# Moving a background chain twelve gather slots later, and packing its last stage into half as many slots

## What is computed

```python
def peer_ffn(x, w_query, sub_keys, u_tab, v_tab):
    q = (xc @ w_query).reshape(PEER_TBLOCK, PEER_HEADS, 2, PEER_QDIM // 2)
    s = jnp.einsum('thcd,ckd->thck', q, sub_keys)
    top_s, top_i = lax.top_k(s, K)                       # K = 16, of 128 keys
    ... best_s, best_j = lax.top_k(cand_s, K)            # of the 256 pair sums
    gate = jax.nn.softmax(best_s, axis=-1)
    act = jax.nn.gelu(jnp.einsum('thkd,td->thk', u_tab[experts], xc))
    v = v_tab[experts]
    return jnp.einsum('thk,thkd->td', (gate * act), v)

def post_norm_block(x, mix, w_out, ...):
    h = layer_norm(ALPHA * x + mix @ w_out, ln1_g, ln1_b)
    return layer_norm(ALPHA * h + peer_ffn(h, ...), ln2_g, ln2_b)

def compress(rows, pe, w1, w2):                          # one of the sparse attention's inputs
    blk = rows[:, idx] + pe[None, None, :, None, :]      # 32 rows, stride 16
    h = jax.nn.gelu(jnp.einsum('bnlgd,lde->bnge', blk, w1))
    return jnp.einsum('bnge,ef->bngf', h, w2)
```

## Time and profile before

| | us |
|---|---|
| median of three runs | 2796.11 |
| profiled execution | 2807.41 |
| its span in the trace | 2805.6 |
| mean granted TensorE clock in it | 0.793 |
| TensorE matmuls busy | 2047.4 (73%) |
| VectorE busy | 1263.4 (45%) |
| GpSimd busy | 796.6 (28%) |
| ScalarE busy | 321.8 (11%) |
| software-issued gathers (q0) | 627.05 MB, 55.2% of the 16 engines' span |
| hardware-issued loads (q1) | 332.46 MB, 31.6% |

### The profile page before, as it was taken

How to read it: one execution, slowest core, us unless ns; L and a number is a source line. 1 busy time by engine, 2 the same in 40 slices (tenths; PEclk the granted TensorE clock), 3 DMA queues, 4 the chain that set the end, 5 groups by cost and what they waited for, 6 DMA issues and landing times.

```text
span 2805.6 us, 30559 instructions
## 1 busy us (share of the span) xinstructions
PE 2047.4 (73%) x10278; PEld 1239.2 (44%) x10278; DVE 1263.4 (45%) x2354; ACT 321.8 (11%) x737; POOL 796.6 (28%) x594
## 2 busy tenths in 40 slices
PE   8999999566979997968998644554544449883334
PEld 5777665234448985746766411211110006550000
DVE  0500121233024785576795525334433354688551
ACT  0001110112012010010011002001001011011011
POOL 0000000000001143443334434225342374436762
PEclk9999999777999998988999875876766655555555
DMA  9789889753425589999999999999999999999997
GB/s 395 290 349 368 343 305 361 284 188 141 189 77 216 208 297 392 373 370 365 388 384 356 354 348 412 389 379 380 414 373 421 422 421 421 421 416 387 422 422 302
DMA packets 213165, 963.81 MB, mean 344 GB/s; under 512 B 23761, under 2 KB 89298, under 8 KB 122258
## 3 DMA queue, kind: packets, MB, share of 16 engines
q0 software_dynamic: 84512, 627.05, 55.2%
q1 hardware_dynamic: 128354, 332.46, 31.6%
q10 hardware_dynamic: 144, 2.36, 0.2%
HBM read 955.28 MB, written 14.88 MB: 346 GB/s over the span
## 4 chain that ended last, share of the span: by engine, by line
PE 44%; DMA 34%; DVE 7%; SPq 7%; issue 4%; POOL 2%; ACT 2%; POOLq 0%; DVEq 0%; ACTq 0%
DMA sb<-in_peer_v,sb 18%; PE bank L861 12%; PE bank L1216 10%; DMA sb<-in_nsa_t 8%; SPq L538 5%; DMA sb<-in_peer_u,sb 5%; PE bank L1441 4%; PE bank L1191 4%; PE bank L1160 4%; PE bank L925 2%; SPq L347 2%; DVE sb L1996 2%; DMA sb<-in_nsa_v 2%; POOL sb L2089 2%; PE bank L965 1%
## 5 line engine op out<-in xcount | busy, mean ns | idle before, releaser
L1996 DVE CUSTOM_DVE_ANT_1 sb<-sb 128x2048 f32<-128x2048 f32 x256 | 585.1, 2292 | 520.5 <-DMA sb<-in_peer_u,sb 516.8
L1441 PE MATMUL bank<-sb 128*32 128x512 f32 x2304 | 477.4, 848 | 422.3 <-DMA sb<-in_peer_v,sb 418.7
L2089 POOL DMA_INDIRECT sb<-in_peer_v,sb x288 | 435.5, 1512 | 665.7 <-PE bank L1441 569.5
L2089 POOL DMA_INDIRECT sb<-in_peer_u,sb x288 | 353.0, 1226 | 630.1 <-DVE sb L1996 360.4
L1216 PE MATMUL bank<-sb 128*128 128x128 f32 x2048 | 467.0, 398 | 65.6 <-DMA sb<-in_nsa_t 65.0
L1216 PEld LDWEIGHTS bank<-sb 128*128 128x128 f32 x2048 | 416.0, 214 | 155.3 <-DMA sb<-in_nsa_t 76.7
L861 PE MATMUL bank<-sb 128*128 128x288 f32 x1408 | 351.2, 409 | 12.6 <-DMA sb<-in_w_in 12.6
L1441 PEld LDWEIGHTS bank<-sb 128*32 128x32 f32 x2304 | 64.8, 126 | 659.7 <-DMA sb<-in_peer_v,sb 601.0
L861 PEld LDWEIGHTS bank<-sb 128*128 128x128 f32 x1408 | 266.6, 191 | 96.2 <-DMA sb<-in_tokens_t 12.6
L835 ACT ACTIVATE sb<-sb 128x32 f32<-128x32 f32 x288 | 85.6, 315 | 836.7 <-PE bank L1441 619.7
L1269 PE MATMUL bank<-sb 128*32 128x512 f32 x128 | 73.7, 743 | 97.8 <-DMA sb<-in_nsa_t 97.8
(11 more groups left out here) (343 smaller groups left out, 1478.2 us busy)
## 6 DMA issues: line engine op xcount, KB each, us to landing
sb<-in_a_k SPq DMA_DIRECT2D x128, 512.0 KB, 6.8
sb<-in_a_v SPq DMA_DIRECT2D x128, 512.0 KB, 6.0
sb<-in_nsa_t SPq DMA_DIRECT2D x384, 128.0 KB, 8.5
sb<-in_w_in SPq DMA_DIRECT2D x44, 1024.0 KB, 9.2
sb<-in_w_out SPq DMA_DIRECT2D x32, 1024.0 KB, 6.0
sb<-in_w_query SPq DMA_DIRECT2D x32, 1024.0 KB, 4.8
sb<-in_nsa_v SPq DMA_DIRECT2D x128, 128.0 KB, 18.1
sb<-in_peer_u,sb POOLq DMA_INDIRECT x288, 15.2
```

What stands on the lines that cost most here:

```text
L1441: mm = pe.matmul(bank[g % 2][32 * c:32 * c + 32, :], diag[j % 4], v_ring[j % 4][:, 512 * c:512 * c + 512], start=(s % 32 == 0), stop=(s % ...
L1996: dve.tensor_tensor_reduce(out=u, in0=u, in1=replica(g), scale=1.0, scalar=0.0, op0=ALU.mult, op1=ALU.add, accum_out=act16[:, r % 2, j:j + ...
L2089: pool.indirect_dma_start(rows[j % 4], None, dram[table], bass.IndirectOffsetOnAxis(ap=idx, axis=0)).then_inc(full[j % 4], 16)
```

## The change

All background pieces start 12 slots later: compression at slot 14 (second half at 66), choice of blocks at 73, attention at 116 and 150, output projection at 191, queries at 224. A query tile takes one slot (16 matmuls) instead of two halves in two slots, so the 16 tiles take slots 224 to 239 instead of 212 to 243. Its score follows four slots after it instead of five after its first half, and stands ahead of the query in its slot. The samples' eight heads are chosen every three slots from slot 232, instead of every four from slot 222; the last expert pair is at slot 254 instead of 251.

```diff
-TAPS_AT = (2, 54)
+TAPS_AT = (14, 66)
-PICK_AT = 61
-NSA_AT = (104, 138)
-OUT_AT = 179
-QUERY_AT = 212
+PICK_AT = 73
+NSA_AT = (116, 150)
+OUT_AT = 191
+QUERY_AT = 224
-        HEADS.update({QUERY_AT + 10 + 4 * h: (2, h) for h in range(NH)})
+        HEADS.update({QUERY_AT + 8 + 3 * h: (2, h) for h in range(NH)})
-        EXPERTS.update({QUERY_AT + 15 + 8 * p: (2, p) for p in range(4)})
+        EXPERTS.update({QUERY_AT + 12 + 6 * p: (2, p) for p in range(4)})
-        GATES.update({QUERY_AT + 20 + 8 * p: (2, p) for p in range(4)})
+        GATES.update({QUERY_AT + 17 + 6 * p: (2, p) for p in range(4)})
@@ ScalarE: one query and one score copied per slot instead of per two slots
-                if d >= 3 and d % 2 == 1:
-                    m = (d - 3) // 2
...
+                if 6 <= d < 22:
+                    m = d - 6
+                    act.wait_ge(s_mm, 16 + m + 1)
...
+                if 2 <= d < 18:
+                    m = d - 2
+                    act.wait_ge(later_used, later_items.used["wq", m])
...
@@ TensorE
-            def query_of(m, half):
...
-                for kt in range(8 * half, 8 * half + 8):
+            def query_of(m):
...
+                for kt in range(KT):
                     mm = pe.matmul(bank[2 + m % 2][:, 0:NSMP], w[:, P * kt:P * kt + P], h_t[:, kt, NPROMPT:T], ...)
-                if 0 <= d < 32:
-                    query_of(d // 2, d % 2)
-                if d >= 5 and d % 2 == 1 and d < 37:
-                    score_of((d - 5) // 2)
+                if 4 <= d < 20:
+                    score_of(d - 4)
+                if 0 <= d < 16:
+                    query_of(d)
```

More of the change, by code:

```diff
@@ L470, in hybrid_step @@
         HEADS.update({40 + 6 * h: (1, h) for h in range(NH)})
-        HEADS.update({QUERY_AT + 10 + 4 * h: (2, h) for h in range(NH)})
+        HEADS.update({QUERY_AT + 8 + 3 * h: (2, h) for h in range(NH)})
         EXPERTS = {2: (0, 1), 7: (0, 2), 14: (0, 3)}
         EXPERTS.update({48 + 12 * p: (1, p) for p in range(4)})
-        EXPERTS.update({QUERY_AT + 15 + 8 * p: (2, p) for p in range(4)})
+        EXPERTS.update({QUERY_AT + 12 + 6 * p: (2, p) for p in range(4)})
         GATE_EXPS = {1: (0, 0), 5: (0, 1), 10: (0, 2), 17: (0, 3)}
         GATE_EXPS.update({50 + 12 * p: (1, p) for p in range(4)})
-        GATE_EXPS.update({QUERY_AT + 17 + 8 * p: (2, p) for p in range(4)})
+        GATE_EXPS.update({QUERY_AT + 14 + 6 * p: (2, p) for p in range(4)})
         GATES = {10: (0, 0), 12: (0, 1), 20: (0, 2), 22: (0, 3)}
         GATES.update({52 + 12 * p: (1, p) for p in range(4)})
-        GATES.update({QUERY_AT + 20 + 8 * p: (2, p) for p in range(4)})
+        GATES.update({QUERY_AT + 17 + 6 * p: (2, p) for p in range(4)})
         EXPERT_FOLDS = {21: (0, 1), 23: (0, 2), 25: (0, 3), 92: (1, 0), 93: (1, 1), 94: (1, 2), 95: (1, 3)}
@@ L804, in background @@
                 d = t - QUERY_AT
-                if d >= 3 and d % 2 == 1:
-                    m = (d - 3) // 2
[L807 to L815, removed]
+                if 6 <= d < 22:
+                    m = d - 6
+                    act.wait_ge(s_mm, 16 + m + 1)
+                    act.activation(s_key[2][0:NSMP, m, :], bank[4 + m % 2][0:NSMP, 0:P], ACT.Copy).then_inc(s_in, 1)
+                if 2 <= d < 18:
+                    m = d - 2
+                    act.wait_ge(later_used, later_items.used["wq", m])
+                    if m >= 2:
+                        act.wait_ge(s_mm, 16 + m - 1)
+                    act.activation(q_t[:, m % 2, 0:NSMP], bank[2 + m % 2][:, 0:NSMP], ACT.Copy).then_inc(q_in, 1)
                 if t == 260:
@@ L1371, in turn_rows @@
                 mm.then_inc(h_turned, 1)
-            def query_of(m, half):
[L1374 to L1380, removed]
-                for kt in range(8 * half, 8 * half + 8):
+            def query_of(m):
+                w = later_arrived(("wq", m))
+                if m == 0:
+                    pe.wait_ge(h_t_in, 9)
+                if m >= 2:
+                    pe.wait_ge(q_in, 16 + m - 1)
+                for kt in range(KT):
                     mm = pe.matmul(bank[2 + m % 2][:, 0:NSMP], w[:, P * kt:P * kt + P], h_t[:, kt, NPROMPT:T], start=(kt == 0), stop=(kt == KT - 1))
-                if half:
-                    mm.then_inc(later_used, 1)
+                mm.then_inc(later_used, 1)
             def score_of(m):
```

## The result

The changed kernel takes 2814.88 us (median of ten runs, 2798.78 to 2820.61), the kernel before beside it 2794.76 (ten runs, 2780.86 to 2805.77). The ratio is 1.0071, 95% interval 1.0051 to 1.0091: about 20 us slower, between 14 and 25. The profiled execution took 2820.61 us (span 2818.8) against 2807.41 (span 2805.6): 13 us more.

What follows compares the result with a forecast made beforehand. After the start DMA, at 0.98 to 1.01, bounds the kernel, so only DMA idle time counts. Start -21.6, taps +15.4, query part +14.2 and VectorE +2 give +10.0: 2796.1 becomes 2806 us, range 2788 to 2820.

Steps and rivals of the forecast that it cites:

- the forecast's own band: Whole kernel: times of 2799 to 2813 us count as the forecast itself, with a chance of 0.45.
- The start, -21.6: Before the first value rows: first v gather no longer behind the VectorE's wait for compression, issued 21.6 us earlier.
- Twelve thirds, +15.4: Twelve more stream slots carry compression taps, at 6.40 us each instead of a plain slot's 5.12: +15.4 us.
- the lower bound, 5.8: Slots with taps: the least cost, TensorE's need of 5.8 us a slot, +8 us for the twelve.
- The query part, +30.8 less 16.6: Sixteen packed query slots become TensorE-bound at half clock, +30.8 us; 16.6 us of DMA work done early comes back.
- The VectorE, +2: After slot 239: heads every three slots need 6.0 us a slot against DMA's 5.12; loss grows by 2 (0 to 9).
- The lead of 3.5 slots from part three: Gathers done ahead during the TensorE-bound query part; claimed to hide most of the VectorE's excess after slot 239.
- The 95 us for slots 240 to 254: After the query part: the VectorE needs some 95 us there against DMA's 77.
- Full clock: Rival: TensorE without gaps gets full clock in the query part, DMA binds, total 0, 2796 us; chance 0.20.
- Faster: Rival: added taps cost only +8, query part and VectorE's excess hidden whole, -13.6, 2782 us; chance 0.15.
- Clearly slower: Rival: the query part's lead gives nothing back, +30.8 in place of +14.2, 2823 us; chance 0.12.
- the last rival: At the start, late u rows replace the wait, so -10 instead of -21.6, 2817 us; chance 0.08.

Runs made afterwards that it cites:

- late sums: Kernel before with only the compression's VectorE sums and later stages three slots later, no tap moved: 2797.06 us against 2790.57, ratio 1.0016.
- shift alone: Kernel before with its background twelve slots later, query tiles still in halves over 32 slots, heads every four: 2781.79 us against 2792.47, ratio 0.9962.
- two with swapped operands: Changed kernel with tokens stationary and weights moving in the query matmuls: ratio 1.0010; the same with heads every four slots, pairs every eight: 0.9975.
- two with dummy matmuls: Changed kernel with four unused 512-column matmuls per query tile, set between its matmuls: ratio 1.0104; grouped behind the tile: 1.0064.
- wide heads: Changed kernel with heads every four slots and pairs every eight instead of three and six: 2805.94 us against 2790.57, ratio 1.0049.
- two with the exponential moved: ScalarE's exponential for slots 224 to 239 at slot 239 instead of 241, in the changed kernel: ratio 1.0084; with heads every four slots too: 1.0078.
- packing alone: Changed kernel with compression back at slot 2, packed queries in slots 212 to 227, heads every three: 2815.52 us, ratio 1.0090.
- shifts by twelve, four and eight: Kernel before with its background twelve, four or eight slots later and nothing else: ratios 0.9962, 0.9973 and 0.9987.
- the two swaps: Query matmul operands swapped in the changed kernel, 1.0071 to 1.0010, and in that with heads every four slots, 1.0049 to 0.9975.
- the two spreads: Heads every four slots, pairs every eight, in the changed kernel, 1.0071 to 1.0049, and in that with swapped operands, 1.0010 to 0.9975.
- the shift by four: Kernel before with its background four slots later and nothing else: 2781.81 us against 2790.69, ratio 0.9973.

## Why the prediction was right, and where its terms were off

The forecast was 2806 us, slower by 10; measured were 2814.88, slower by 20 (14 to 25). That is inside the range (2788 to 2820) but above the forecast's own band (2799 to 2813). Sign and mechanism were right; two terms of the sum, the query part and the VectorE behind it, were too small: together 16.2 us, where the runs give 25 and the profiles 27 to 29.

**The start, -21.6.** Value rows at 1005.47 where 1005.4 was forecast, no wait for the sums, TensorE idle for 35.66 us (36). That the first fits to 0.1 us is luck: the gather went out at 998.19, not 995.8, and landed after 7.3 us instead of 9.6. What the late sums add is that the wait was only half of it: some of the thirds have to leave the front too. Four gone give 17.7 of the 21.5 us, so most of the twelve were not needed for it.

**Twelve thirds, +15.4.** In the two profiles the stretch up to the query part grew by 47.8 us for twelve slots, or 47.8 + 21.5 = 69.3 without the start's gain: 5.78 a slot, which would be TensorE's own need (the lower bound, 5.8), not 6.40. But the 46 slots compared with the earlier trace rows say 6.56, and two profiles can't decide a term of 7 us. The nine profiles whose code is the same up to there (shift alone, the changed kernel, two with swapped operands, two with dummy matmuls, wide heads, two with the exponential moved) reach their first query between 2347.8 and 2374.8 us, and packing alone, with the code of before up to there, at 2296.2 where the kernel before has 2314.8. By the means, 2359.8 and 2305.5, twelve slots cost 54.3 + 21.5 = 75.8 us, 6.3 a slot, give or take about 1, so the forecast's 6.40 may well have been right. By the runs, start and taps together make -11 us (-18 to -4) in the shift alone and -7 as the mean of the shifts by twelve, four and eight; forecast was -21.6 + 15.4 = -6.2. Whether the twelve-slot shift gains more than forecast stays open.

**The query part, +30.8 less 16.6.** A slot with a score takes 2415.42 - 2405.70 = 9.72 us from value rows to value rows, 0.34 more than the 9.38 forecast; the 0.44 us in which the query waits for the ScalarE was not in the sum. (The ScalarE copies the query of two tiles before only when the score in front of it in the slot is done.) The part took 152.0 us against 148.5 forecast. At 370 GB/s it moved 56.2 MB; its 32 gathers and 16 weights of 1.05 MB are 50.3, so by this estimate 5.6 gathers were done ahead (6.5 forecast), 14.1 us of DMA work. The part then lost 152.0 x (1 - 370/421) = 18.4 us of DMA time, forecast 14.2.

**The VectorE, +2.** Behind the query part the changed kernel loses 73.7 x (1 - 381/421) = 7.0 and 97.4 x (1 - 401/421) = 4.6 us, the shift alone 0 and 92.5 x (1 - 407/421) = 3.1. That is 8.5 us more, not 2: 3.2 are the hand-over with the v ring full, which I hadn't seen, the rest stands where the VectorE is busy throughout. This is the term that was mis-sized most, and the step behind it is "The lead of 3.5 slots from part three hides most of it". The price of a slot on the VectorE was right. Thirteen dot products in a row, the first and the last of them here, stand 72.48/12 = 6.04 us apart, and 6.0 was forecast:

```profile
2518.42 2.29 DVE L1992 CUSTOM_DVE_ANT_1 sb<-sb 128x2048 f32<-128x2048 f32 x1
...
2590.90 2.29 DVE L1992 CUSTOM_DVE_ANT_1 sb<-sb 128x2048 f32<-128x2048 f32 x1 [0.18 <-DVE sb L1766]
```

(The 95 us for slots 240 to 254 don't follow from it, though: 15 x 6.0 is 90, an excess of 13 over DMA's 77 and not 18.) What was wrong is the hiding. The lead is landed rows; the VectorE still has to work through them, and its own work of those slots on top, while new u gathers wait for it.

**The sum.** 18.4 + 8.5 = 27 us for the packing, where the forecast's terms give 14.2 + 2 = 16.2; the profiles' 50 slots say 28.7 (323.1 - 294.4), the runs 25 (16 to 34). With the shift's -7 to -11 that makes 14 to 20, and 20 was measured. What the experiments leave less sure is the split of these 27: TensorE 17 and 21 us by the two swaps, VectorE 6 and 10 by the two spreads, all with some 9 us either way, and in the batch with the exponential moved the spread heads gained nothing sure (1.0078 against 1.0084).

**The rivals.** Full clock fell: 0.50 throughout. Its price for a tile was nearly right, though: where the dummies had raised the clock a quarter tile took 1.01 us instead of 1.75, 0.58 of it. The Trainium skill's rule that sustained busy time releases the throttle (TensorE: Matmul & The Clock Gate, "The HAM clock gate") does not hold for this stretch, 146.7 busy of 152.0 us at 0.50. Faster fell with it. Clearly slower, 2823, had u gathers held by v gathers and "the VectorE waits for scores" as its mechanism. Both happened in part. The u gathers did stand behind the v gathers, and the VectorE waited for scores twice, 6.78 us until 2418.52 and 6.39 until 2437.96 (waits in the changed kernel, 2362 to 2640 us: total, times, longest):

```profile
DVE sb L1721 <- ACT sb L808: 13.2, 2, 6.8
```

A lead was built all the same, but only part of it paid. The 32 slots took 152.0 + 73.7 = 225.7 us against 199.6: of the 30.8 us only 30.8 - 26.1 = 4.7 were given back by slot 255, less than the 18 from which I let this rival decide. The median lies halfway between it and the forecast, which its chance of 0.12 did not reflect. The start moved, so the last rival fell.

## What to carry to other kernels

Ask of each stage which engine has room before packing work into it: the query tiles were hidden while they were spread over slots that DMA bounded, and packing them and their heads cost 25 us. A lead that a stall builds up is worth its bytes only once, less the hand-over in which a full ring leaves DMA idle, and only if the engine that must consume it has time to spare. A wait seen on an engine is no gain by itself, twice here: the sums moved without the taps gained nothing, and neither did the exponential. And before a term of some 10 us is read from where a stage ends, look at a second profile: here the same code differed by up to 27 us.

## What the runs showed of the hardware

- The mean granted clock of the sixteen query slots in four kernels, of which three kept TensorE busy for 96% or more of the time: 0.50 with query matmuls of 32 moving columns at 96.5% busy, 0.66 with the swapped ones at 67.4 of 120.6 us (56%), 0.92 with 512-column matmuls set between (153.53 of 159.3 us busy), 0.63 with the same ones grouped (143.04 of 148.3).
- One matmul can cost as much as four: a single 512-column matmul between query tiles took 0.97 us, four of them one after the other, each into its own group of 32 columns, took 1.06 as value rows at full clock (in the rows of the shift by four).
- The same 16 products took 7.01 us with 128 weight columns loaded for 32 moving ones, and 1.94 us the other way round, spread over four groups of 32 columns. The one more matmul that adds the four parts takes 0.64 us. Which of the two, the order or the groups, gives how much was not tried apart.
